# Expert order by a bit-reversed place in a mixture-of-experts kernel, in place of a listed permutation

## What is computed

```python
logits = hf @ w_router + b_router            # 512 tokens x 32 experts
top_val, top_idx = lax.top_k(logits, 4)      # each token goes to 4 experts
gates = softmax(top_val)
for each expert e, for each block of its rows:
    gu  = xb @ w_gu[e] + b_gu[e]             # 1024 -> 2048
    act = (clip(up) + 1) * (gt * sigmoid(1.702 * gt))
    out = (act @ w_down[e] + b_down[e]) * gate
    y[rows] += out
x = x + gt_f * y;  return rmsnorm(x, g_final)
```

## Time and profile before

| | us |
|---|---|
| median of 3 runs | 1492.36 |
| the runs | 1489.11, 1492.36, 1493.59 |
| the profiled execution, its own time | 1493.59 |
| its span in the trace | 1491.7 |
| experts: end of item 0 to end of item 44 | 333.95 to 1459.34 |

### The profile page before, as it was taken

One profiled execution on the slowest core, in us unless ns is written; L12 is line 12 of the kernel. 1 busy time (PEld: TensorE's weight loads), 2 busy tenths in 40 slices (PEclk: granted clock), 3 DMA queues, 4 the chain that ended last, 5 costly groups with the idle time before them and its releaser, 6 DMA issues.

```text
span 1491.7 us, 25997 instructions
## 1 busy us (share of the span) xinstructions
PE 1326.8 (89%) x6235; PEld 536.1 (36%) x6235; DVE 905.7 (61%) x1451; ACT 648.5 (43%) x724; POOL 254.4 (17%) x156
## 2 busy tenths in 40 slices
PE   4699879589999999999879987799999999999991
PEld 2587458533333333333223322233332333333330
DVE  2899886755556565555445543555555556565555
ACT  3333742234544444454334433345444544445443
POOL 1741253211111111111110100111111111111111
PEclk9799979589999999999999999999999999999996
DMA  9665222789999999699999999999997299999993
GB/s 379 227 212 207 101 111 80 280 279 372 380 380 380 378 390 376 198 375 382 382 385 377 385 380 381 386 384 364 382 381 258 62 380 382 377 384 377 393 383 136
DMA packets 207765, 477.51 MB, mean 320 GB/s; under 512 B 18562, under 2 KB 19074, under 8 KB 206722
## 3 DMA queue, kind: packets, MB, share of 16 engines
q1 hardware_dynamic: 196914, 458.39, 82.9%
q0 software_dynamic: 10832, 18.90, 5.6%
HBM read 464.11 MB, written 20.45 MB: 325 GB/s over the span
## 4 chain that ended last, share of the span: by engine, by line
PE 45%; SPq 26%; DVE 8%; DMA 8%; issue 8%; ACT 3%; POOL 1%; DVEq 1%; ACTq 0%; POOLq 0%
PE ps L1498 23%; SPq L320 20%; PE ps L1510 9%; DMA ring<-in_w_down 6%; SPq L323 4%; DVE window L1037 2%; DMA wm<-in_w_mod 2%; PE ps L1314 2%; PE ps L1315 2%; PE ps L1316 2%; PE ps L1490 1%; PE ps L1480 1%; PE ps L1402 1%; PE ps L1403 1%; PE ps L1404 1%
## 5 line engine op out<-in xcount | busy, mean ns | idle before, releaser
L1498 PE MATMUL ps<-window,xT 128*64 128x512 f32 x2880 | 645.9, 597 | 27.1 <-DVE window L1037 19.1
L1037 DVE COPY window<-ring 128x2048 f32 (+1 forms) x364 | 444.3, 1227 | 315.7 <-PE ps L1510 104.3
L1510 PE MATMUL ps<-window,aT 128*64 128x512 f32 x1440 | 340.8, 602 | 30.9 <-DVE window L1037 18.5
L759 ACT ACTIVATE window<-ring 128x2048 f32 x180 | 340.0, 1908 | 50.6 <-DMA ring<-in_w_down 38.0
L1498 PEld LDWEIGHTS ps<-window,xT 128*64 128x64 f32 x2880 | 196.4, 137 | 406.3 <-issue 349.5
L753 ACT ACTIVATE sg<-gb 128x256 f32<-128x256 f32 x90 | 37.5, 416 | 424.2 <-DVE gb L1184 424.2
L563 POOL DMA_INDIRECT y_rows<-osb,idx_c x46 | 78.0, 1695 | 633.9 <-ACT osb L749 619.4
L1510 PEld LDWEIGHTS ps<-window,aT 128*64 128x64 f32 x1440 | 90.6, 136 | 187.5 <-issue 133.4
L1184 DVE TENSOR_SCALAR gb<-ps 128x256 f32<-128x256 f32 x90 | 38.2, 424 | 170.7 <-PE ps L1498 170.7
L550 POOL DMA_INDIRECT xg<-h_rows,idx_n x46 | 65.3, 1420 | 412.2 <-DVE idx_n L1074 386.6
L749 ACT ACTIVATE osb<-ps,gate_c 128x512 f32<-128x512 f32 x46 | 31.7, 688 | 119.9 <-PE ps L1510 119.2
(11 more groups left out here) (292 smaller groups left out, 1166.8 us busy)
## 6 DMA issues: line engine op xcount, KB each, us to landing
ring<-in_w_gate_up SPq DMA_DIRECT2D x512, 512.0 KB
ring<-in_w_down SPq DMA_DIRECT2D x128, 1024.0 KB
wm<-in_w_mod SPq DMA_DIRECT2D x4, 2048.0 KB, 21.8
wm_a<-in_w_mod SPq DMA_DIRECT2D x4, 2048.0 KB, 9.1
wm_b<-in_w_mod SPq DMA_DIRECT2D x4, 2048.0 KB, 8.7
win<-in_w_in SPq DMA_DIRECT2D x3, 2048.0 KB, 20.1
x_in<-in_x SPq DMA_DIRECT2D x1, 2048.0 KB, 10.7
wo_f<-in_w_out SPq DMA_DIRECT2D x1, 2048.0 KB, 7.8
```

Of the source, the lines that this page charges most:

```text
L759: A(window[c % NW][:, :, :, :], ring_chunk(c, p), ACT.Copy).then_inc(S["moved_by_act"], 1)
L1037: V.tensor_copy(window[c % NW][:, :, :, :], ring_chunk(c, p)).then_inc(S["moved_by_dve"], 1)
L1498: last = MMUL(ps[M * j:M * (j + 1), h, :].rearrange("m (g n) -> m g n", g=2), xT[:, k, :], window[c % NW][:, k % CK, :, j * GW:(j + 1) * G ...
L1510: last = MMUL(ps[M * y:M * (y + 1), 2, :], aT[:, h, i, M * j:M * (j + 1)], window[c % NW][:, k % CK, y, :], start=False, stop=(h == 1 and ...
```

## The change

The listed permutation is taken out, and the place of rank r (0 to 30) becomes the number r + 1 with its five bits in reverse order. Expert 0 still gets place 0. Nothing else differs: the number of instructions, the loads, their sizes and their number are the same.

```diff
-PLACE_OF_RANK = (23, 8, 13, 3, 26, 5, 18, 20, 28, 16, 11, 1, 9, 27, 29, 17, 12, 21, 14, 10, 24, 6, 22, 31, 4, 7, 2, 25, 15, 30, 19)
...
-    put("place", np.array([*PLACE_OF_RANK, 0])[None])
+    put("place", np.array([int(f"{r:05b}"[::-1], 2) for r in [*range(1, NE), 0]])[None])
```

## The result

The changed kernel takes 1504.80 us (median of 4 runs, 1503.15 to 1507.58) against 1490.80 us for the kernel before beside it: 14.0 us more, ratio 1.0097 (95% interval 1.0084 to 1.0109). The forecast was 14.8 us more. The profiled execution took 1505.6 us, span 1503.7, 12.0 us more than the profiled execution of before. Over all executions of the two kernels on record, which weren't all taken beside each other, the medians are 1505.92 (23 of them) and 1493.36 us (48): 12.6 us more. So 14.0 may be a little high.

What follows compares the result with a forecast made beforehand. TensorE's items and the weight loads were taken to bound the kernel in turn. Four new short rests of 3.7 us add 14.8 us to the median of 1492.36, giving 1507.2 us, range 1501 to 1512.

Steps and rivals of the forecast that it cites:

- What bounds the kernel: Expert part: TensorE's items (24.33 us each) and weight loads (D, 34.6 us an expert) take turns; 54.9 us of TensorE stalls.
- the long and short rests: Load stream pausing at a full ring: long 17.8 and 42.1 us ahead of loads 9 and 17, four short of 3.8.
- The order of items by rank: Items by place in the new expert order: eight late first items, 70.7 us of stalls against 55.5.
- Each us of rest more is a us more of time: Weight-load stream: the last load sets the end, so rests of 75.1 against 59.9 us cost 15.2 us.
- The price of a short rest: Ahead of loads 3, 5, 19 and 21: 3 x 24.33 - 2D each, taken as 3.7 us, 14.8 us for four.
- The shortest distance of two late items: Read in the trace of before as 34.36 us a load, giving a rest of 4.3 us and the upper bound 17.1.
- the rival of a quicker stream: Weight loads speed up under the new order, deciding from D = 33.6 on; at 33.0 the time is 1477; chance 0.02.
- Waits on line 443 longer by about 15 us: Expected sign in SyncE's load queue: its waits on this line grow by about 15 us in sum.
- The signs of being wrong: Loads at another distance than 34.5 to 34.8 us, or items 3 to 10 already waiting (ceiling under 20).
- The rival of fast transfers: Loads so fast that both orders run at TensorE's pace, 1492 us; within the 0.05 for no change.
- the rule: Expert part: a load's lead changes by -10.3, +14.1, +38.4 or +62.7 us for 1 to 4 items, between zero and the ceiling.
- The ceiling near 20: Largest lead the 16-chunk ring allows, taken as 20.6 us; at 30 the orders would differ by only 1.6 us.

Runs made afterwards that it cites:

- e5: Before and changed orders, from load 2 on 12 of the chunks bring one of two slices (6 MB an expert): 1439.91 and 1439.60 us, ratios 0.9639 and 0.9642.
- e1: Changed order with four pairs of neighbouring places swapped, leaving no short rests: ratio 0.9999 to the kernel before.
- e4: Order of before with the 22 experts of one item reversed among their places, items by place the same: ratio 1.0010 to before.
- e2: Order of before with places 2 and 3, 4 and 5 swapped, giving two short rests at the head: ratio 1.0037 to before.
- e9: Changed order with places 2 and 3, 4 and 5 swapped, leaving two short rests behind the four-item expert: ratio 1.0043 to before.
- e3: Kernel before with all seven two-item experts at places 2, 4 to 14, giving seven short rests: 1.21% slower, ratio 1.0121.
- e10: Gathers and scatters moved out of range in the orders of before, of the change and with seven short rests: 1460.77, 1452.35, 1478.40 us; ratios 0.9777, 0.9717, 0.9901.

## Why the prediction was right, and what was off in it

**What bounds the kernel: right.** Two streams, an item of 24.33 us and a load of about 34.5, and the end set by the load stream's rests. With shorter loads both orders take the same time (e5), and the long and short rests are seen at the loads where they were put.

**The order of items by rank: right.** The late items are the eight that were forecast, 11, 17, 21, 22, 35, 39, 40 and 44, and a ninth of 0.48 us (item 10), 66.4 us in sum against 70.7.

**Each us of rest more is a us more of time: right in direction and place.** Zero, two, two, four and seven short rests cost -0.1, 5.5, 6.4, 14.0 and 18.1 us, and the four loads at which the change was to rest, 3, 5, 19 and 21, are the ones with the longer issue. Nothing else in the change costs anything (e1, e4, e5).

**The price of a short rest, 3 x 24.33 - 2D with D = 34.65: a little too high, for D isn't one number.** It was 3.7 us; the runs give 2.8 (e2), 3.2 (e9), 3.5 (changed; 3.1 over all executions on record) and 2.6 (e3). The formula fits with another D, and that D is the term off is the reading that I hold the likelier; that a part of each rest, 0.2 to 1.1 us, is filled by chunks in flight would lower the price in the same way, and no run excludes it. I took D from the distances of load starts, 34.54 and 34.71, for the whole stream. By the late items it is 32.3 us plus 0.018 for each row gathered or scattered beside it, so it runs from 32.4 to 34.5 in the rows at hand. A two-item expert brings many rows, and where it makes a rest D is higher (35.6 by the line for the 183 rows in e2) and the rest shorter; the rows are the same in number in every order, so what a load takes more in one place it takes less in another, and the total follows the rests. With D by the line the four rests of the change come to 13.3 us, against 14.8 forecast and 14.0 measured. The bounds of the forecast, 12.0 to 17.1, held. That the one number 3.7 came so near is in part luck: the rests of the change stand beside 128 to 153 rows, and beside the 132 to 186 rows of e3 the same number missed by 8 us. Full hiding by chunks in flight (cost 0) and an extra slot wait at each rest are both out.

**The shortest distance of two late items: misread.** I gave it as 34.36 and said that no stretch in the rows is below it. But the earlier trace rows has 933.95 to 967.65, 33.70 us, and I had listed that item myself, late by 9.37. With it a rest would have been 5.6 us and the upper bound 22.4, and the rival of a quicker stream would have lacked its main objection. It was also the sign in the trace of before that D isn't one number.

**Waits on line 443 longer by about 15 us: wrong.** They are 188.4 us against 143.1, 45 more. The issue of load 3 alone is 4.8 us longer than in the earlier trace rows, beside a rest of 2.6 to 3.9 in the transfer engines. The queue seems to wait for slots also while chunks issued earlier are still on their way (this is argued); its waits are no measure of the stream's rests. The share and the rate of the transfer engines in a window come nearer.

**The signs of being wrong.** Item 10 did wait, by 0.48 us, which I had named as the sign of a ceiling under 20. By my own numbers its expert, at place 7, has a lead of 20.6 - 2 x 10.3 = 0.0, so a few tenths on D are enough and the sign was drawn too sharply. Loads at another distance than 34.5 to 34.8 was the other sign. By their starts they keep to it in long stretches (loads 24 to 31 of the changed kernel begin 242.3 us apart, 34.6 each); by the distances of late items they don't (33.83 and 33.03).

**The rival of fast transfers: the sign was missed.** It said that both orders would be equal, and put the stalls of the order of before at D = 30 at about 3 us, where the rule gives 6. At 30.5 and at 32.05 the changed order is 12 and 8 us *faster*, for it has no run of more than three singles. The rule had this in it; I had worked it out for too few values of D. The rival that begins there, a quicker stream, is then real, but not in this kernel: it needs 2 us less for each load. The ceiling near 20 was right within 2 us or so (e10 fits 22 better): with 30 the loss would not have been there.

**A version that beats both** was looked for with the rule, over orders of the same items: none has less than the 55.5 us of the order of before, since the two long rests can't be avoided by order and short ones can only add. No run beat it. That is the rule's answer, not a proof on the chip.

## What to carry to other kernels

Where a prefetch ring feeds work of uneven length, keep the book of two streams: how far each unit's load is ahead, with a floor at zero (the consumer waits) and a ceiling at the ring's size (the producer rests). A rest of the producer costs nothing when it happens and is paid in full later if the producer's total sets the end, so long units should stand just far enough apart that the lead never meets the ceiling; even spacing by a formula knows nothing of the ceiling, and which order is best turns with the ratio of load to work. Take the load's length from several distances between units that both came late, in the stage in question, with the other traffic of that stage in it, and look at the shortest and the longest and not only at the mean.

## What the runs showed of the hardware that was not expected

The rows that the items gather and scatter lengthen the weight loads beside them: 34.4 us with 64 rows in and 64 out, 32.05 with none, by the line about 0.018 us for each row. The bytes alone don't say so. The queue of these transfers moves 18.90 MB in all, and 2.16 MB with all rows out of range: (18.90 - 2.16) / 46 = 0.36 MB for each of the 46 pairs, 0.9 us at the loads' 393 GB/s, where the line has 2 x 2048 x 0.018 / 45 = 1.6 us for an item on average. Per byte these transfers cost the stream nearly twice what weights do. The time of their packets says the same: it is 5.6% of the transfer engines' span in the kernel before, 83.5 us, and 0.8%, 11.7 us, in e10_quiet_before, which is 71.8 / 46 = 1.6 us for each pair. With them gone, and the experts' part missing from the output, the kernel of before is 2.2% faster, more than the order of the experts is worth in this change.
